# Turns of sixteen tokens and eight early steps in the gate stage, in place of eight and four

## The reference, cut to what matters

```python
sv, pos = lax.top_k(cand, PEER_TOPK)            # 8 heads, 16 experts each, per token
eidx = jnp.take_along_axis(cidx, pos, axis=-1)  # expert = 128 * i1 + i2
gate = jax.nn.softmax(sv, axis=-1)
u = u_tab[eidx]
act = jax.nn.gelu(jnp.einsum('thkd,td->thk', u, xc), approximate=False)
w = gate.astype(act.dtype) * act
vv = v_tab[eidx]
return jnp.einsum('thk,thkd->td', w, vv)
```

## Time and profile before

| | |
|---|---|
| median of three runs | 3929.72 us (3929.45 to 3932.48) |
| profiled execution, its own time | 3930.48 us |
| its span, first to last instruction | 3928.7 us |
| TensorE busy | 3786.8 us, 96% |
| VectorE busy | 2783.4 us, 71% |
| GpSimd busy | 2532.8 us, 64% |
| ScalarE busy | 750.4 us, 19% |
| mean granted clock of TensorE | 0.988 |
| the gate stage, layer 1 and 2 | about 641 to 906 us, 2586 to 2854 us |

### The profile page before, as it was taken

One profiled execution on the slowest core, in us unless ns is written; L12 is line 12 of the kernel. 1 busy time (PEld: TensorE's weight loads), 2 busy tenths in 40 slices (PEclk: granted clock), 3 DMA queues, 4 the chain that ended last, 5 costly groups with the idle time before them and its releaser, 6 DMA issues.

```text
span 3928.7 us, 54215 instructions
## 1 busy us (share of the span) xinstructions
PE 3786.8 (96%) x19024; PEld 3130.0 (80%) x19024; DVE 2783.4 (71%) x3945; ACT 750.4 (19%) x1297; POOL 2532.8 (64%) x1268
## 2 busy tenths in 40 slices
PE   6999999999999999999989999999999999999998
PEld 5778887778878888888877798877788878888886
DVE  7545998996999744444585459989959996444445
ACT  1551112331111111111115411123311111111111
POOL 5445577546777767676654455865467877767664
PEclk9999999999999999999999999999999999999999
DMA  3112234777454433333222223357764453333332
GB/s 145 54 65 98 91 140 156 231 228 245 182 203 181 145 123 115 120 128 117 86 88 73 79 87 106 133 177 228 229 237 180 186 193 129 118 128 117 117 117 75
DMA packets 229056, 555.03 MB, mean 141 GB/s; under 512 B 10048, under 2 KB 141376, under 8 KB 179392
## 3 DMA queue, kind: packets, MB, share of 16 engines
q1 hardware_dynamic: 46656, 335.57, 23.7%
q10 hardware_dynamic: 182272, 217.75, 16.9%
HBM read 446.32 MB, written 106.95 MB: 141 GB/s over the span
## 4 chain that ended last, share of the span: by engine, by line
PE 72%; DVE 18%; issue 6%; POOL 2%; DVEq 1%; ACT 1%; DMA 0%; ACTq 0%; POOLq 0%; SPq 0%
PE bank L1085 23%; PE bank L1087 22%; PE bank L1086 22%; DVE Wl L1018 3%; DVE hot L986 2%; DVE hot2l L991 2%; DVE hot L987 2%; DVE Wf L1014 2%; DVE X L1035 1%; POOL part_l L383 1%; POOL part_h L380 1%; PE bank L1211 1%; PE bank L1364 1%; PE bank L1406 1%; PE bank L1199 1%
## 5 line engine op out<-in xcount | busy, mean ns | idle before, releaser
L383 POOL TENSOR_TENSOR part_l<-landing,part_h 128x1024 fp32r<-128x1024 f32 x632 | 1715.5, 2714 | 52.7
L380 POOL TENSOR_SCALAR part_h<-landing 128x1024 fp32r<-128x1024 f32 x632 | 828.0, 1310 | 1309.0 <-PE bank L1087 756.8
L1085 PE MATMUL bank<-XTh,part_h 128*128 128x512 f32 (+1 forms) x2688 | 1054.0, 392 | 15.2 <-DVE XTl L711 7.7
L1087 PE MATMUL bank<-XTh,part_l 128*128 128x512 f32 (+1 forms) x2688 | 1038.4, 386 | 0.0
L1086 PE MATMUL bank<-XTl,part_h 128*128 128x512 f32 (+1 forms) x2688 | 1038.3, 386 | 0.0
L1085 PE MATMUL bank<-part_h,Wh 128*128 128x512 f32 x2048 | 801.0, 391 | 11.1 <-DVE X L1035 8.2
L1087 PE MATMUL bank<-part_h,Wl 128*128 128x512 f32 x2048 | 797.4, 389 | 0.0
L1086 PE MATMUL bank<-part_l,Wh 128*128 128x512 f32 x2048 | 797.1, 389 | 0.0
L1085 PEld LDWEIGHTS bank<-XTh,part_h 128*128 128x128 f32 x2688 | 509.5, 190 | 116.7 <-issue 7.7
L1087 PEld LDWEIGHTS bank<-XTh,part_l 128*128 128x128 f32 x2688 | 508.6, 189 | 102.6
L1086 PEld LDWEIGHTS bank<-XTl,part_h 128*128 128x128 f32 x2688 | 509.9, 190 | 96.3
(11 more groups left out here) (165 smaller groups left out, 3522.5 us busy)
## 6 DMA issues: line engine op xcount, KB each, us to landing
landing<-stream SPq DMA_DIRECT2D x316, 1024.0 KB, 4.8
dense_gates<-spill ACTq DMA_DIRECT2D x32, 2048.0 KB, 9.2
gate<-dense_gates ACTq DMA_DIRECT2D x64, 1024.0 KB, 4.8
early_acts<-early ACTq DMA_DIRECT2D x144, 256.0 KB, 2.3
acts_in<-early_acts ACTq DMA_DIRECT2D x36, 1024.0 KB, 7.4
LNP<-ln ACTq DMA_DIRECT2D x5, 1024.0 KB, 4.9
X<-x SPq DMA_DIRECT2D x4, 512.0 KB, 9.9
keyT<-keys ACTq DMA_DIRECT2D x2, 1024.0 KB, 4.8
```

Of the source, the lines that this page charges most:

```text
L380: nc.gpsimd.tensor_scalar(part_h[k][:, w], landing[s][:, w], 1.0, 0.0, ALU.mult, ALU.add).then_inc(high_part, 1)
L383: nc.gpsimd.tensor_tensor(part_l[k][:, w], landing[s][:, w], part_h[k][:, w].bitcast(F32), ALU.subtract).then_inc(split.sem, 1)
L1085: nc.tensor.matmul(dst, sth, mvh, start=first, stop=False)
L1087: return nc.tensor.matmul(dst, stl, mvh, start=False, stop=last)
```

## The change

TensorE's turn becomes twice as long: it waits for two slots at once, makes the gates of sixteen tokens, then takes eight early steps. The slots, their number and all other engines stay as they are. The count of instructions stays the same but for half of the waits for `hots`.

```diff
                     for q in range(16):
-                        if q % 2 == 0:
-                            pe.wait_ge(hots.sem, hots.at(l, 8 * b + (q // 2 + 1)))
+                        if q % 4 == 0:
+                            pe.wait_ge(hots.sem, hots.at(l, 8 * b + (q // 2 + 2)))
                         if not (first and q < 4):
                             pe.wait_ge(gate_copied.sem, gate_copied.at(l, 16 * b + (q - 3)))
...
                         ins.then_inc(gated.sem, 1)
-                        if q % 2 == 1:
-                            for j in range(4):
-                                early_product(E_BEFORE + q // 8, 2 * b, 4 * (q // 2 % 4) + j, False)
+                        if q % 4 == 3:
+                            for j in range(KD):
+                                early_product(E_BEFORE + q // 8, 2 * b, KD * (q // 4 % 2) + j, False)
```

## The result

The changed kernel takes 3937.64 us (median of 16 runs, 3935.63 to 3942.59), the kernel before 3929.65 us beside it (16 runs, 3928.02 to 3933.11): a ratio of 1.0021, 95% interval 1.0014 to 1.0029, so slower by some 8 us. The profiled execution has a span of 3938.0 us, 9.3 more than before. It took 3939.78 us in all, 2.1 above its kernel's median, while the profiled one of the kernel before lies 0.8 above its own; so what is read from these two profiles overstates the usual difference by some 1.3 us.

A forecast was written before the change was run, and what follows sets the result against it. VectorE was taken to bound the gate stage, with TensorE having slack. Delays of 5.9 us in the first layer and 3.3 in the second sum to 9.2; on the median of 3929.72 that gives 3938.9 us, range 3933 to 3944.

The forecast's parts named there:

- The opening: Start of each layer's gate stage: VectorE waits 0.7 us at unit 7, 2.4 at unit 9; net 2.2 and 2.3 us.
- the steady round: Gate stage, four units: TensorE waits about 1.5 us per 16.3 us round, VectorE goes without a break; nothing gained or lost.
- the two ends: Last set of each layer's gate stage has two units to do after the last wait: ends 5.9 and 3.3 us later.
- VectorE bounds the stage: Gate stage: VectorE sets the pace at 261.5 us a layer; TensorE needs 239.4 and has slack.
- Rival (c): Gate stage: TensorE's turns set the pace, so fewer switches and slow units save some 12 us, 3917; chance 0.07.
- the saving of 0.07 us a set: TensorE's set of two units takes 7.41 us instead of 7.48 by fewer switches; counted only in each layer's last set.
- the half-clock stretches did multiply: Named sign against the prediction: TensorE's half-clock stretches in the gate stage multiply or vanish.
- the return to y = 2.9: Steady gate stage: units ready when a split begins return to 2.9 whatever the number before, against four slots.
- rival (d): End of each layer's gate stage: a split slips past the last unit, 5.86 us less each, 3927; chance 0.05.
- rival (b): Opening and last set: longer idling costs TensorE clock, up to 6.4 us more, 3942 to 3945.3; chance 0.15.
- The delay passes on in full: Behind the gate stage TensorE is at its bound, so the stage's whole delay, 9.2 us in sum, reaches the total.

The follow-up runs named there:

- light_short: Kernel before, but VectorE makes no hot2l and TensorE multiplies hot2h twice; 3883.28 us against 3930.08 beside it, ratio 0.9884.
- slots8: Changed kernel with eight slots for VectorE's tiles in place of four; 3935.96 us, ratio 1.0017 to the kernel before.
- wait_each: Changed kernel, but TensorE waits for each slot by itself instead of two at once; 3936.35 us, ratio 1.0018 to the kernel before.
- end_long: Kernel before with only the last 64 tokens of each layer in the new long turns; 3932.32 us, ratio 1.0007.
- light_long: Changed kernel, but VectorE makes no hot2l and TensorE multiplies hot2h twice; 3888.93 us, ratio 0.9899 to the kernel before.
- open_long: Kernel before with only the first 64 tokens of each layer in the new long turns; 3936.2 us, ratio 1.0017.
- both_short: Changed kernel with the first and last 64 tokens of each layer in the old turns; 3932.33 us, ratio 1.0008 to the kernel before.

## Why the prediction was right

The forecast was 3938.9 us, 9.2 above before; measured are 8.0 (ratio 1.0021) and 9.3 of span. The opening came as worked out; the steady round did not, and the two ends came out by sums whose errors cancel. Point by point:

**VectorE bounds the stage: shown.** light_short takes 46.8 us off by a VectorE operation alone. Rival (c), TensorE's turns, falls with it. Its one true part, the saving of 0.07 us a set, came to 0.09.

**The opening: as worked out.** Waits of 0.7 and 2.4 us were forecast at units 7 and 9, and 0.69 and 2.36 are there; set 2 was to begin 20.8 us after VectorE's first operation and begins at 20.7. slots8 shows that the ring of four makes them. The double wait is only a small part of it: wait_each still has 2.2 us of the 3.0.

**The steady round: wrong.** The prediction had TensorE wait 1.5 us in every round and never a stall of VectorE. In fact it waits 1.6 to 3.1 us every second or third round, seven sets behind such a wait run at the lower clock, and in the second layer VectorE stalls once, 1.0 us. Five later units ran slow before, so the half-clock stretches did multiply, which the prediction had named as a sign against it. The step that failed is the return to y = 2.9 whatever it was before. It treats a split as one whole unit of VectorE, and y under 3. But the split starts a little after the round's end (the next set begins at 765.25, the split at 765.61), so y is 3.0, and VectorE's operations come one by one. This is GpSimd's first operation of that split, then VectorE's timeline beside it, units 31 (first row) and 32 (the last row but one):

```profile
765.61 1.48 POOL L380 TENSOR_SCALAR part_h<-landing 128x1024 fp32r<-128x1024 f32 x1 [6.43 <-PE bank L1087]
...
764.89 0.68 DVE L991 TENSOR_TENSOR hot2l<-hot,wtl 128x1024 f16<-128x1024 f16 x1
765.49 0.69 DVE L986 TENSOR_TENSOR hot<-iota,idx 128x1024 f16<-128x1024 f16 x1
766.09 1.53 DVE L987 TENSOR_TENSOR hot<-iota,idx 128x1024 f16<-128x1024 f16 x1
767.74 2.69 DVE L990 TENSOR_TENSOR hot2h<-hot,wth 128x1024 f16<-128x1024 f16 x1
770.36 1.53 DVE L991 TENSOR_TENSOR hot2l<-hot,wtl 128x1024 f16<-128x1024 f16 x1
771.81 2.87 DVE L986 TENSOR_TENSOR hot<-iota,idx 128x1024 f16<-128x1024 f16 x1
```

The unit's first operation slips in ahead of the split, three are slowed, and the unit is ready 6.3 us after the split's start instead of some 8.5. TensorE has no wait in this round, VectorE falls back by 0.6 unit in it (14.8 us less 5.9 for the split are 3.4 units, and four are taken), and the wait comes later and larger. The even round exists, in wait_each, where the first unit of a set need not wait for the second. On average the pace is still VectorE's, so the steady part added little to the sum; what it changed is when TensorE and the splits come to the end.

**The end: the forecast path in the second layer only, and two terms whose errors cancel.** First layer: forecast 5.9, measured 4.2. The forecast had TensorE wait for the last unit; it waited last for the set of units 55 and 56, before this row of its timeline, ran that set slow (8.9 us) and the next ones without a wait:

```profile
872.45 0.28 PE L1406 MATMUL bank<-hot2h,hot 128*128 128x128 f16 x1 [3.02 <-DVE hot2l L991]
```

The last unit was ready 261.40 us after VectorE's first operation, as before, though it had waited 3.0 us. About 0.9 of that lay in a split, and the last split was still running when the last unit was done (902.84 of 896.49 to 905.07), so some 2.2 us of it cost VectorE nothing. This is rival (d), in part and in one layer. The last set began 0.7 us after the unit was ready, so an earlier unit would have gained nothing more; end_long and slots8, where the split slipped past the last unit in both layers, show that the price of rival (d), 5.86 us less a layer, does not hold. Second layer: forecast 3.3, measured 5.2. The last unit was ready 2.6 us later (2.3 forecast; VectorE waited a third time, 1.0 us, behind a set that ran 10.1 us at the lower clock), and the last set, after a wait of 2.15 us, took some 9.0 us instead of 7.4, its granted clock 0.63 in the first 4 us. This is rival (b), in one layer. 1.7 less and 1.9 more leave the sum where it was, by luck rather than by the steps.

**The delay passes on in full: shown** by the lengths, which hold all 9.3 us, while the rest takes the same time within 0.2 us.

The Trainium skill (Perfetto Trace Analysis, Matmul Optimizations) asks for matmuls back to back in batches. The traces agree in this, that work behind some waits was granted 0.50 to 0.67 of the clock, and work without waits all of it. They don't show that longer batches gain clock: the 0.09 us a set in light_long are won at a granted clock of 1.00 in both kernels, and where TensorE waits for VectorE, the longer batches made the waits longer (up to 3.1 us for 2.37 in the steady part) and the slow stretches more, seven for five.

**What stays open.** Which waits are followed by the lower clock: those of 3.0 us at 741.5 and 3.1 at 2805.2 were, one of 3.1 at 839.7 was not (its set took 7.39), and of the waits of 2.1 us the one at the end of the second layer was, two others were not. The parts do not add up exactly either (open_long and end_long are 6.9 and 4.2 us in the lengths, the whole 9.4), since each shift moves the phase of splits and waits. The ratios carry some 3 to 3.5 us of uncertainty either way (6 in light_short and light_long), so no single part is measured better than that, and how much the steady part costs, between nothing and the 3.5 us of both_short, stays open.

## What to carry to other kernels

Where an engine waits for another and then does a turn of mixed work, the end of the stage is the last wait plus all that stands behind it. The last wait need not be the one for the last piece of data: look for it in the trace. Making turns longer saves switches only if that engine is the bound; if it is the waiting one, put the independent work ahead of the wait, not behind it. Check the opening and the last turn by themselves: the steady part may cost little while the opening and the end cost most of it. A round whose phase is tenths of a microsecond from a threshold should not be trusted to settle: take both outcomes into the range.

## What the runs showed of the hardware

A VectorE operation of 0.68 us that starts beside a running GpSimd operation takes 1.5 or 2.7 to 2.9 us, until some 0.5 us after that operation ends: one VectorE operation per GpSimd operation. In the first layer of the kernel before, 64 units take 261.4 us where 64 x 2.62 are 167.7: 93.7 us lost in sixteen splits, 5.9 each. An operation already begun when GpSimd starts is not slowed (0.69 us at 765.49, with GpSimd starting at 765.61). So the place of a split among the four operations decides when a unit is ready, by 2 us, though the loss stays the same.

In the changed kernel TensorE's granted clock fell to 1.2 GHz behind waits of 9.3 us, behind six of 3.0 to 3.1 us and one of 2.15, and a set of 7.39 us then took 8.8 to 10.1 us; behind one wait of 3.1 us, two of 2.1 and one of 1.6 it did not. In the kernel before it fell behind five of nine waits of 2.3 to 2.4 us.
